# A hybrid attention encoder block on eight cores: eight buffers for x, weight loads queued behind it, a reordered last attention unit, per-block waits in the output projection, and the last tile's norm in pieces

## The chip, the cores and the metric

The kernel runs on one Trainium2 chip, on all 8 NeuronCores at once, with one program. Each core takes half of the 2048 tokens of one of four sequences as its own (1024 output rows) and reads the whole sequence for keys and values; no core talks to another. The metric is device time in microseconds of the slowest core.

## The reference

`x` is (4, 2048, 2048) float32; there is one layer. What is computed:

```python
h = rms_norm(x, norm_gain)
qa, ka, va, ga, qb, kb, vb, gb, za, zb = split(h @ w_in)      # 11776 columns
# A: 8 query heads, 2 key/value heads of 128, dense softmax attention over 2048 keys
qa, ka = axial_rotary(rms_norm(qa)), axial_rotary(rms_norm(ka))
pa = (gqa_attention(qa, ka, va) * silu(ga)) @ w_branch_a
# B: 3 groups of 4 heads, window/dilation (128,1), (512,4), (2048,16), partial rotary,
#    groups combined by their softmax denominators
pb = (dilated_mixture(rotary(qb), rotary(kb), vb) * silu(gb)) @ w_branch_b
merged = sigmoid(za + b0) * pa + sigmoid(zb + b1) * pb
y = rms_norm(x + merged @ w_out, final_norm_gain)
```

## The kernel before, in words

**Stages.** (1) Head: the transposed x comes in 16 tiles of 1 MB (`xload`, tile g = 4s+q holds 512 tokens of slice s and four of the 16 blocks of 128 channels). ACT squares each tile, four matmuls with a matrix of ones sum the squares (`head_sums`), ACT makes rsqrt by Ln and Exp, and 16 DVE operations per slice write the normalised bf16 `hT` (`head_scale`). (2) `kv_proj` projects keys (32 matmuls of 512 columns per slice) and values (64 matmuls of 256 columns per slice), and `rope_post` normalises and rotates each key or query slice. (3) Mixer A (`projA`, `attA_S`, `attA_PV`, `attA_sum`), eight heads. (4) Mixer B (`projB`, `attB_S`, `attB_PV`), twelve units of one head slot and one group; the last one is n = 11. (5) Merge (`merge_units`): for each of 16 blocks c, za, zb, wba and wbb projections into the eight PSUM banks, two sigmoids, products and a sum into `mergedT` block c. (6) Output (`out_mm`): 8 token tiles by 4 column blocks, 16 matmuls each over the blocks k of `mergedT`, then the residual add, the squares and `final_norm`.

**What sets the order.** A class `Sched` records each operation into its engine's instruction list and works out the semaphore waits from named keys; `Streams.run` (line 290) merges generators, each a stream of small steps, always taking the one whose next operation its own cost model has ready earliest, less the stream's bonus (sums 0.6, scale 0.5, posts 0.3, kv 0.1, PVB 0.06, SB 0.05, projections `pj_bonus`). So the order on every engine is fixed when the program is built, and an engine waits in that order at run time. In the model every DMA costs its source bytes over 330 GB/s plus 2 us.

**Buffers of x.** `xbs` has five (NXB = 5): two halves of `yaT`, `ybT`, `gain`, and columns 10752 to 12800 of the arena ("xb4"). Tile g+5 is loaded when `head_scale` has used tile g. All x loads, the constants and both rotary tables (1 MB each, keys "ropeC", "ropeS") are issued on SP's queue at the start; weights are issued on POOL (`w_issue`, 1 MB read as float32 and written as 512 KB of bf16, eight slots). The first four wait for x tiles 1, 2, 3, 3 (`w_issue(xbk[g])`), and two more (qa0, ga0) follow at once since `projA` asks for them; slots 6 and 7 hold the squares during the head. The matrix of ones is part of `cbf`, a constant of 336 KB loaded on POOL ahead of the weights.

**Around the end of mixer B.** `proj_all` runs `projA`, `projB` and then `merge_head`, which projects za and zb of block 0 into banks 0, 1, 2 and 7; bank 7 is taken only when the last epilogue of B (`epB` = 4) is planned. After `X.run()` come the sigmoids and `mu0[14:]`, which starts with wba of block 0.

**Output.** Each matmul of `out_mm` names all 16 keys of `mergedT` (`mkeys`), though it reads one block. `final_norm` is a DVE reduction of four sums, ACT Ln and Exp, and two DVE operations of 1024 columns, each followed by a 512 KB store on SP; the program ends by waiting for the last four stores.

## Time and profile before

| | |
|---|---|
| median of 3 runs | 1216.16 us (1214.97 to 1318.25) |
| profiled execution | 1222.34 us |
| its span, slowest core (core 5) | 1220.8 us |
| spans of the cores | 1210.8 to 1220.8 us |
| PE / DVE / ACT busy on core 5 | 1158.3 / 605.1 / 510.3 us |
| last matmul of core 5 over | 1212.5 us |

The profile is one execution; its times are from the start of the span. What the device adds around the span is 1222.34 - 1220.8 = 1.5 us. "PE" is the matmul side of TensorE, "PEld" its weight loads, "idle before" the engine's idle time ahead of a group with what ended it. The granted clock is a share of 2.4 GHz.

### The profile page before, as it was taken

The numbers are of one execution on the slowest core, as the hardware profiler recorded it, in microseconds if no ns is written. First come the engines' busy times: TensorE is split into PE (matmuls) and PEld (weight loads), VectorE is DVE, ScalarE is ACT, GpSimd is POOL, SyncE is SP. The second block draws the span as 40 slices with busy tenths as digits, with TensorE's granted clock in tenths as the row PEclk, the third lists the DMA queues.
The fourth block names the chain that finished last, engine by engine and source line by source line (L and its number), as shares of the span: only waits on it lengthen the run. The fifth ranks groups of instructions, "written<-read, shape, count | busy, mean of one in ns | idle before, by whom it ended". The sixth has DMA issues, their size and how long they took to land.

```text
span 1220.8 us, 17436 instructions; the slowest of 8 cores (1210.8 to 1220.8 us)
## 1 busy us (share of the span) xinstructions
PE 1158.3 (95%) x5876; PEld 548.2 (45%) x5876; DVE 605.1 (50%) x904; ACT 510.3 (42%) x899; POOL 79.3 (6%) x165
## 2 busy tenths in 40 slices
PE   2779999999999999999999999999999999999997
PEld 0325644444444554455454454444444444434442
DVE  0559587878877653555554646332212122122254
ACT  3345477877787643443543544221111111102222
POOL 1000100000000000000000000001111111010000
PEclk9869999999999999999999999999999999999998
DMA  9945442211132423321322330036666545349333
GB/s 233 261 141 136 72 68 35 36 30 26 33 70 36 87 38 55 65 53 35 70 53 38 67 61 5 8 60 110 106 107 111 89 75 91 67 114 250 80 139 137
DMA packets 27174, 102.15 MB, mean 84 GB/s; under 512 B 3408, under 2 KB 5456, under 8 KB 23504
## 3 DMA queue, kind: packets, MB, share of 16 engines
q0 software_dynamic: 20304, 63.27, 31.2%
q1 hardware_dynamic: 6784, 37.78, 9.2%
q8 instruction: 49, 0.80, 0.3%
q14 instruction: 37, 0.30, 0.1%
HBM read 155.90 MB, written 8.39 MB: 135 GB/s over the span
## 4 chain that ended last, share of the span: by engine, by line
PE 86%; DVE 5%; DMA 5%; issue 2%; ACT 2%; DVEq 0%; SPq 0%; ACTq 0%
PE pb L218 86%; DVE s_arena L218 2%; DVE s_hT L218 2%; DMA s_arena<-xt 2%; DMA s_gain<-xt 2%; DMA s_yaT<-xt 1%; ACT s_arena L218 1%; DVE s_gain L218 1%; ACT s_wsl L218 0%; ACT s_rs L218 0%; SPq L218 0%; DVEq L1319 0%; ACT s_gain L218 0%; DVEq L216 0%; DVE s_yaT L218 0%
## 5 line engine op out<-in xcount | busy, mean ns | idle before, releaser
L218 PE MATMUL pb<-s_hT,s_wsl 128*128 128x512 bf16 (+1 forms) x3456 | 754.7, 371 | 4.9 <-DVE s_hT L218 2.4
L218 PEld LDWEIGHTS pb<-s_hT,s_wsl 128*128 128x128 bf16 x3456 | 329.9, 98 | 382.0 <-issue 24.4
L218 ACT ACTIVATE s_arena<-pb 128x512 bf16<-128x512 f32 (+8 forms) x514 | 285.4, 577 | 287.0 <-PE pb L218 232.0
L218 DVE TENSOR_TENSOR s_arena<-pb,s_arena 128x512 f32<-128x512 f32 x96 | 77.6, 809 | 267.2 <-PE pb L218 265.2
L218 PE MATMUL pb<-s_arena 128*128 128x512 bf16 (+3 forms) x746 | 154.3, 310 | 5.2 <-DVE s_arena L218 3.1
L218 ACT ACTIVATE s_arena<-pb,s_mb 128x512 f32<-128x512 f32 x64 | 43.7, 687 | 241.8 <-PE pb L218 241.8
L218 DVE TENSOR_TENSOR s_arena<-s_arena 64x512 bf16<-64x512 f32 (+2 forms) x144 | 111.4, 773 | 19.3 <-ACT s_arena L218 12.8
L218 POOL DMA_DIRECT2D s_wsl<-w_in x92 | 48.6, 529 | 924.4 <-PE pb L218 904.5
L218 PEld LDWEIGHTS pb<-s_arena 128*128 128x128 bf16 x746 | 62.7, 98 | 65.6 <-issue 12.4
L218 DVE TENSOR_TENSOR s_arena<-s_arena,s_rope 128x512 f32<-128x512 f32 (+3 forms) x136 | 89.9, 661 | 4.1 <-DVE s_arena L218 0.2
L218 DVE TENSOR_TENSOR s_gain<-s_gain,s_arena 128x512 f32<-128x512 f32 x89 | 61.5, 691 | 22.2 <-ACT s_arena L218 15.6
L218 DVE COPY s_arena<-pb 128x512 f32<-128x512 f32 (+3 forms) x56 | 35.7, 637 | 70.4 <-PE pb L218 70.0
L218 PE MATMUL pb<-s_hT,s_arena 128*128 128x512 bf16 x256 | 61.6, 408 | 0.0
L218 PE MATMUL pb<-s_wsl,s_cbf 128*128 128x512 bf16 x64 | 25.6, 545 | 34.6 <-ACT s_wsl L218 20.9
L218 PE MATMUL pb<-s_yaT,s_wsl 128*128 128x512 bf16 x256 | 57.9, 379 | 0.0
L218 ACT ACTIVATE s_arena<-s_arena 128x512 f32<-128x512 f32 x80 | 50.3, 634 | 16.0 <-DVE s_arena L218 12.9
L218 ACT ACTIVATE s_gain<-pb 128x512 bf16<-128x512 f32 x86 | 50.2, 601 | 10.4 <-PE pb L218 10.2
L218 DVE TENSOR_TENSOR s_arena<-pb,s_rope 64x512 f32<-64x512 f32 (+1 forms) x64 | 40.8, 638 | 22.1 <-ACT s_arena L218 21.3
L218 PE MATMUL pb<-s_arena,s_cbf 128*128 128x512 bf16 (+1 forms) x158 | 47.7, 337 | 4.1 <-DVE s_arena L218 3.4
L218 DVE TENSOR_TENSOR s_gain<-s_gain 128x512 f32<-128x512 f32 (+2 forms) x59 | 40.7, 690 | 12.9 <-ACT s_gain L218 6.6
L218 PEld LDWEIGHTS pb<-s_hT,s_arena 128*128 128x128 bf16 x256 | 26.5, 103 | 34.8 <-issue 19.7
L218 PEld LDWEIGHTS pb<-s_yaT,s_wsl 128*128 128x128 bf16 x256 | 25.0, 98 | 30.2
(65 smaller groups left out, 599.3 us busy)
## 6 DMA issues: line engine op xcount, KB each, us to landing
s_wsl<-w_in POOLq DMA_DIRECT2D x92, 512.0 KB, 6.2
y<-s_arena SPq DMA_DIRECT2D x16, 512.0 KB, 2.7
s_yaT<-xt SPq DMA_DIRECT2D x7, 1024.0 KB, 8.6
s_wsl<-wba POOLq DMA_DIRECT2D x16, 256.0 KB, 4.9
s_hT<-xr SPq DMA_DIRECT2D x4, 1024.0 KB, 16.6
s_hT<-wout POOLq DMA_DIRECT2D x8, 512.0 KB, 34.2
s_ybT<-xt SPq DMA_DIRECT2D x3, 1024.0 KB, 14.2
s_gain<-xt SPq DMA_DIRECT2D x3, 1024.0 KB, 17.4
```

What stands on the lines that cost most here:

```text
L218: ins = getattr(engine, fn[0])(**fn[1])
```

## The change

Head: three more x buffers, two in the part of `hT` that holds slice 3 (each 8 blocks of 256 float32 columns, pieces of 1 KB) and one in columns 6144 to 8192 of the arena ("xb5", later the gate buffers of mixer A), with explicit tables of buffers and successors. The matrix of ones is a tile of its own set by DVE; `cbf` and the merge bias are loaded after x tile 15. Weights: two behind tiles 2 and 3, two behind tile 5, and qa0 and qa1 behind tiles 13 and 15. The rotary table comes in four pieces, one per slice, with a key each. `projA` starts after tile 9 (before: 7), takes qa0, qa1, then ga0, ga1, and the rest as before. End of B: the bonus of the projections falls to -0.15 once `pj_n` is over 19.75; `merge_head` also projects wba of block 0, with banks 3 and 4 taken after the last scores and bank 7 after the last PV instead of after the epilogue. Output: `out_mm` names `("mT", k)` alone. Last tile: the product with the gain is made ahead of the norm in four pieces, the sum of the four sums goes by an ACT copy with accumulation, and the scaling goes in four pieces of 512 columns, two on ACT and two on DVE, each with a 256 KB store. In the diff, `["cbf"]` becomes `["ones"]` wherever the matrix of ones is read, and "ropeC"/"ropeS" become `("rope", t0 // 512)` in the posts (left out below).

```diff
+        ones_t = sb("s_ones", [128, 128], BF16)
-        for h in range(8):
-            wlist.append((("qa", h), wsrc(w_in, QA0 + h * 128), 16))
-            wlist.append((("ga", h), wsrc(w_in, GA0 + h * 128), 16))
+        for nm, base, h in [("qa", QA0, 0), ("qa", QA0, 1), ("ga", GA0, 0), ("ga", GA0, 1)] + \
+                [(nm, base, h) for h in range(2, 8) for nm, base in (("qa", QA0), ("ga", GA0))]:
+            wlist.append(((nm, h), wsrc(w_in, base + h * 128), 16))
...
-        xbs += [g4(gain[:]), g4(af(10752, 12800))]
-        xbk += [["gain"], ["xb4"]]
-        NXB = len(xbs)
+        xbs.append(g4(gain[:]))
+        xbk.append(["gain"])
+        for i in range(2):
+            xbs.append(hT[:, 8 * i:8 * i + 8, 1536:2048].bitcast(F32))
+            xbk.append([("hT", k, 3) for k in range(8 * i, 8 * i + 8)])
+        xbs += [g4(af(10752, 12800)), g4(af(6144, 8192))]
+        xbk += [["xb4"], ["xb5"]]
+        XBUF = (0, 1, 2, 3, 6, 7, 4, 5, 0, 1, 2, 3, 6, 7, 0, 1)
+        XNEXT = {max(j for j in range(g) if XBUF[j] == XBUF[g]): g for g in range(8, 16)}
...
+        def rope_load(s):
+            sl = slice(512 * s, 512 * (s + 1))
+            S.dma("sp", rope[:, :, sl], ropeA_d.rearrange("a p t -> p a t")[:, :, sl], "c_rope%d" % s, writes=[rope_all[s]])
...
-        S.dma("pool", cbf[:], cbf_d, "c_cbf", writes=["cbf"])
-        for g in range(NXB):
-            xload(g)
-        for g in (1, 2, 3, 3):
-            w_issue(xbk[g])
+        MEMSET(ones_t[:], 1.0, ["ones"], eng="dve")
+        for g in range(4):
+            xload(g)
+        w_issue(XK[2])
+        w_issue(XK[3])
+        xload(4)
+        xload(5)
+        rope_load(0)
+        w_issue(XK[5])
+        w_issue(XK[5])
+        xload(6)
+        xload(7)
+        rope_load(1)
...
-                    if g + NXB < 16:
-                        xload(g + NXB)
+                    if g in XNEXT:
+                        xload(XNEXT[g])
+                        X.setf(("xl", XNEXT[g]))
+                    if g == 5 or g == 9:
+                        rope_load(2 if g == 5 else 3)
+                    if g == 9:
+                        w_issue(XK[13])
+                        w_issue(XK[15])
+                        S.dma("sp", mb[:], mb_d, "c_mb", writes=["mb"])
+                        S.dma("pool", cbf[:], cbf_d, "c_cbf", reads=XK[15], writes=["cbf"])
...
         def pj_bonus():
+            if pj_n[0] > 19.75:
+                return -0.15
             return 0.5 if pj_n[0] < at_n[0] + 1.15 else 0.0
...
         def projA():
-            yield from ge("sc", 8)
-            for h in range(8):
-                if h == 1:
-                    yield from ge("sums_done", 1)
-                    yield from ge("kv_done", 1)
+            yield from ge("sc", 10)
+            for nm, h in [("qa", 0), ("qa", 1), ("ga", 0), ("ga", 1)] + [(nm, h) for h in range(2, 8) for nm in ("qa", "ga")]:
+                if (nm, h) == ("ga", 0):
+                    yield from ge("kv_done", 1)
+                    yield from ge("sums_done", 1)
...
         def merge_head():
-            for i, nm in enumerate(("za", "zb")):
+            for i, nm in enumerate(("za", "zb", "wba")):
...
                 for s in range(2):
                     bi = ZB[i][s]
+                    pool = "pj" if bi < 3 else "S"
                     if bi == 7:
-                        yield from ge("epB", 4)
-                        yield from X.take("O", bi)
-                    else:
-                        yield from X.take("pj", bi)
-                    yield from mm16(w, s * 512, 512, bi, 0.1)
+                        continue
+                    if pool == "S":
+                        yield from ge("SB_done", 12)
+                    yield from X.take(pool, bi)
+                    yield from merge_mm(nm, w, s, bi)
+                    yield
+                if i == 1:
+                    yield from ge("PB_done", 12)
+                    yield from X.take("O", 7)
+                    yield from merge_mm(nm, w, 1, 7)
                     yield
...
             for k in range(16):
                 MM(pb[bi][:], mergedT[:, k, t * 128:(t + 1) * 128], wbig[cb][:, k, :], (k == 0), (k == 15),
-                   mkeys + [("wb", cb, k // 4)], [PS(bi)])
+                   [("mT", k), ("wb", cb, k // 4)], [PS(bi)])
...
+        def pre_gain(t, cb):
+            sl = slice(cb * 512, (cb + 1) * 512)
+            TT(ost[t % 2][:, sl], xts[t][:, sl], gain[:, sl], ALU.mult, [("xp", t, cb), "gain"], [("ost", t % 2, cb // 2), ("og", cb)])
+
+        def last_norm(t):
+            sc = stat[:, 32 + t:33 + t]
+            ACT(stat[:, 48:52], stat[:, 4 * t:4 * t + 4], AF.Copy, [("fs", t, cb) for cb in range(4)], [("fd", t)], accum_out=sc)
+            ACT(sc, sc, AF.Ln, [("fd", t), "eps"], [("fd", t)], scale=1.0 / D, bias=eps_t[:, 0:1])
+            ACT(sc, sc, AF.Exp, [("fd", t)], [("fd", t)], scale=-0.5)
+            for cb in (0, 2, 1, 3):
+                o = ost[t % 2][:, cb * 512:(cb + 1) * 512]
+                if cb < 2:
+                    ACT(o, o, AF.Copy, [("og", cb), ("fd", t)], [("og", cb)], scale=sc)
+                else:
+                    S.op("dve", "tensor_scalar", dict(out=o, in0=o, scalar1=sc, scalar2=None, op0=ALU.mult),
+                         [("og", cb), ("fd", t)], [("og", cb)])
+                otoks.append(S.dma("sp", y[t * 128:(t + 1) * 128, cb * 512:(cb + 1) * 512], o, "outl_%d" % cb, reads=[("og", cb)]))
+
-        for t in range(8):
+        for t in range(7):
             out_mm(t, 2)
             out_mm(t, 3)
             final_norm(t)
-        for tk in otoks[-4:]:
+        pre_gain(7, 0)
+        pre_gain(7, 1)
+        out_mm(7, 2)
+        pre_gain(7, 2)
+        out_mm(7, 3)
+        pre_gain(7, 3)
+        last_norm(7)
+        for tk in otoks[-8:]:
```

## Rows read from the trace of the kernel before

**Rows 1.** The page: busy tenths of PE in 40 slices of 30.5 us, core 5.
```profile
PE   2779999999999999999999999999999999999997
```
**Rows 2.** Stretches: length, busy time (instructions) by engine, granted clock, DMA share, GB/s.
```profile
0.00:125.00 125.00, 86.66 (x383) 38.71 (x384) 66.10 (x99) 58.36 (x63) 5.25 (x15) 0.89 0.69 188
125.00:400.00 275.00, 269.83 (x1323) 125.24 (x1321) 211.32 (x325) 202.74 (x378) 12.78 (x26) 1.00 0.27 45
...
783.00:800.00 17.00, 14.04 (x85) 6.38 (x84) 7.86 (x11) 3.93 (x7) 0.53 (x1) 0.91 0.18 32
...
1085.00:1098.00 13.00, 10.44 (x42) 4.24 (x40) 4.06 (x6) 0.69 (x1) 4.23 (x8) 0.87 0.67 183
```
**Rows 3.** PE's groups by shape, from 0 to 125 us.
```profile
L218 PE MATMUL pb<-s_wsl,s_hT 128*128 128x256 bf16 x146 | 17.1, 273 | 0.0
```
**Rows 4.** The chain that ended last: start us, us, what.
```profile
3.83 23.20 DMA s_arena<-xt
...
41.37 19.02 DMA s_gain<-xt
...
95.69 8.57 DMA s_yaT<-xt
...
796.14 293.67 PE pb L218 x1352
```
**Rows 5.** Stretches of 10 us in the head, columns as in rows 2.
```profile
60.00:70.00 10.00, 8.57 (x19) 2.36 (x20) 5.98 (x10) 3.27 (x4) 0.00 (x0) 0.50 0.22 73
70.00:80.00 10.00, 7.42 (x32) 2.68 (x29) 4.71 (x8) 4.79 (x4) 0.00 (x0) 1.00 0.86 275
80.00:90.00 10.00, 6.56 (x16) 2.13 (x17) 5.84 (x9) 7.33 (x8) 0.00 (x0) 0.51 0.25 75
```
**Rows 6.** Weight loads to landing: the six of 14 to 23 us, then the one of 105 us.
```profile
DMA to landing us min/median/max: 11.6/15.2/29.0
...
s_wsl<-w_in POOLq DMA_DIRECT2D x1, 512.0 KB, 5.2
```
**Rows 7.** Instructions of ACT and DVE in the head, in order of time.
```profile
20.46 1.91 ACT L218 ACTIVATE s_wsl<-s_gain 128x2048 bf16<-128x2048 f32 x1 [1.75 <-DMA s_gain<-xt]
27.22 1.91 ACT L218 ACTIVATE s_wsl<-s_arena 128x2048 bf16<-128x2048 f32 x1 [4.85 <-DMA s_arena<-xt]
29.03 0.67 ACT L218 ACTIVATE s_rs<-pb,s_eps_t 128x512 f32<-128x512 f32 x1
...
30.60 5.39 DVE L218 SCALAR_TENSOR_TENSOR s_hT<-s_yaT,s_gnt,s_rs 128x512 bf16<-128x512 f32 x8 [30.60 <-ACT s_rs L218]
...
98.18 0.74 DVE L218 SCALAR_TENSOR_TENSOR s_arena<-pb,s_qkg,s_arena 128x512 f32<-128x512 f32 x1
...
101.87 0.74 DVE L218 SCALAR_TENSOR_TENSOR s_arena<-pb,s_qkg,s_arena 128x512 f32<-128x512 f32 x1
```
**Rows 8.** PE's and ACT's instructions at the end of mixer B.
```profile
793.90 0.38 PE L218 MATMUL pb<-s_arena,s_cbf 128*128 128x512 bf16 x1 [1.10 <-DVE s_arena L218]
796.09 2.59 ACT L218 ACTIVATE s_arena<-s_arena 128x512 f32<-128x512 f32 x4 [7.34 <-DVE s_arena L218]
796.14 4.07 PE L218 MATMUL pb<-s_hT,s_wsl 128*128 128x512 bf16 x11 [1.86 <-DVE s_arena L218]
```
**Rows 9.** The first matmuls of the output projection.
```profile
1094.07 4.13 PE L218 MATMUL pb<-s_rope,s_arena 128*128 128x512 bf16 x11 [2.56 <-DVE s_arena L218]
```
**Rows 10.** DVE's last operations.
```profile
1212.58 0.69 DVE L218 TENSOR_TENSOR s_yaT<-pb,s_yaT 128x512 f32<-128x512 f32 x1 [2.70 <-PE pb L218]
...
1215.20 2.48 DVE L218 SCALAR_TENSOR_TENSOR s_arena<-s_yaT,s_stat,s_gain 128x1024 f32<-128x1024 f32 x2 [0.85 <-ACT s_stat L218]
```
**Rows 11.** The page's DMA issues: the stores of y, KB each, median us to landing.
```profile
y<-s_arena SPq DMA_DIRECT2D x16, 512.0 KB, 2.7
```
**Rows 12.** Stretches near the end: core 0's first, then core 5's, columns as in rows 2.
```profile
1180.00:1190.00 10.00, 10.00 (x48) 4.53 (x47) 5.44 (x8) 3.24 (x10) 0.00 (x0) 1.00 0.61 204
...
1200.00:1210.00 10.00, 10.00 (x40) 4.16 (x39) 5.41 (x7) 1.97 (x7) 0.00 (x0) 0.81 0.37 149
```

More of the change, by code:

```diff
@@ L372, in build_nc @@
         ident = cbf[:, 0:128]
-        ones_bf = cbf[:, 128:256]
+        ones_bf = ones_t[:]
         maskF = cbf[:, 256:768]
@@ L479, in rk @@
             return rope_all
-        rope_all = ["ropeC", "ropeS"]
+        rope_all = [("rope", s_) for s_ in range(4)]
         def g4(ap2d):
@@ L529, in head_sums @@
                     g = 4 * s + q
-                    yield from ge("xl", g + 1 - NXB)
-                    ACT(sqs[g % 2], xbs[g % NXB], AF.Square, xbk[g % NXB], [("w", 6 + g % 2)])
+                    yield from X.until(lambda: g < 8 or ("xl", g) in X.flags)
+                    n = XB[g].shape[2]
+                    ACT(sqs[g % 2] if n == 512 else sqs[g % 2].rearrange("p k (u n) -> p (k u) n", n=n), XB[g], AF.Square, XK[g],
+                        [("w", 6 + g % 2)])
                     yield
@@ L534, in head_sums @@
                         MM(pb[bank][:], ones_bf, sqs[g % 2][:, j, :], (q == 0 and j == 0), (q == 3 and j == 3),
-                           [("w", 6 + g % 2), "cbf"], [PS(bank)], inc=(j == 3))
+                           [("w", 6 + g % 2), "ones"], [PS(bank)], inc=(j == 3))
                     yield
@@ L589, in rope_post @@
             b2 = yield from X.alloc("pj")
-            MM(pb[b2][:], ones_bf, sqv[i], True, True, [("sq", i), "cbf"], [PS(b2)])
+            MM(pb[b2][:], ones_bf, sqv[i], True, True, [("sq", i), "ones"], [PS(b2)])
             X.free("sq", i)
@@ L741, in attA_S @@
         def attA_S():
-            yield from ge("sc", 15)
+            yield from ge("sc", 13)
             for i in range(4):
@@ L820, in attA_PV @@
                         if kc not in DSET:
-                            MM(pb[7][:], ones_bf, pbufs[p], pe_first, False, ["cbf", ("pbuf", p)], [PS(7)], inc=True)
+                            MM(pb[7][:], ones_bf, pbufs[p], pe_first, False, ["ones", ("pbuf", p)], [PS(7)], inc=True)
                             pe_first = False
@@ L1086, in attB_PV @@
                         lb = yield from X.alloc("O")
-                        MM(pb[lb][:], ones_bf, P_, True, True, ["cbf", pk], [PS(lb)])
+                        MM(pb[lb][:], ones_bf, P_, True, True, ["ones", pk], [PS(lb)])
                         X.free("pb", p)
@@ L1206, in build_nc, with merge_mm @@
         TKEYS = [(a, j) for a in ("swp", "bt1", "bt2", "sgb") for j in range(2)] + [("pbuf", i) for i in range(4)]
+        def merge_mm(nm, w, s, bi):
+            if nm != "wba":
+                yield from mm16(w, s * 512, 512, bi, 0.01)
+                return
+            for k in range(8):
+                MM(pb[bi][:], w[0][:, k, :], yaT[:, k, s * 512:(s + 1) * 512], (k == 0), (k == 7), [w[1]] + yakeys, [PS(bi)],
+                   inc=(k % 4 == 3))
+                if k == 3:
+                    yield
         def merge_head():
-            for i, nm in enumerate(("za", "zb")):
+            for i, nm in enumerate(("za", "zb", "wba")):
                 w = W((nm, 0), 3)
@@ L1250, in build_nc @@
         mu0 = merge_units(0)
-        for f in mu0[14:]:
+        for f in (mu0[16], mu0[18]) + tuple(mu0[19:]):
             f()
@@ L1275, in build_nc @@
                 big_piece(cb, q)
-        mkeys = [("mT", c) for c in range(16)]
         ost = [af(8192, 10240), af(10240, 12288)]
```

65 lines of the change are left out of this document (34 added, 31 removed).

## The prediction
> **What bounds the kernel now.** I read the busy slices first. PE is at 9 tenths or more in every slice but the first three and the last [rows 1], so from about 90 us on the kernel is a row of matmuls, and time can be won only where PE stands or runs slowly. The price of a matmul comes from the longest undisturbed piece of the chain: 1352 in 293.67 us [rows 4], 0.217 us for 512 columns. One of 256 columns is 17.1 us over 146, 0.117 us [rows 3]. Then the stretches. From 0 to 125 us PE did 383 matmuls [rows 2], 146 of them short: 237 x 0.217 + 146 x 0.117 = 51.4 + 17.1 = 68.5 us of work. So 56.5 us of the first 125 are lost, to idleness and to the lower clock (0.50 and 0.51 granted in two of the slices of 10 us, that is the level of 1.2 GHz, each after PE had waited [rows 5]). From 125 to 400 us PE is idle for 5.2 of 275 us [rows 2], with DVE busy for 211 and ACT for 203. Two small holes are left, at 793 to 800 us [rows 8] and at 1091 to 1098 us [rows 9], and the tail: the last add of DVE starts at 1212.58 us [rows 10] and the span ends at 1220.8.
>
> In the head the chain goes through the transfers of x: 23.2 us for the fifth tile, 19.0 us for one of the second round, 8.57 us for the last, which lands at 104.3 us [rows 4]. Yet the DMA engines are only 0.22 and 0.25 busy in 60 to 70 and 80 to 90 us, and 0.86 between [rows 5]: five buffers let the stream stop, since tile g+5 waits until tile g has been scaled.
>
> **Head, the stream.** From 70 to 80 us 275 GB/s moved at a busy share of 0.86 [rows 5], 320 GB/s when full, so a tile of 1.05 MB costs 3.28 us. The second-round tile of [rows 4] landed at 60.4 us, and by then nine tiles, both rope tables (two more of that size), cbf (about 2 us) and six weights had gone through, from about 2 us on: 60.4 - 2 - 2 - 11 x 3.28 = 20.3 us, 3.4 us a weight. After the change, ahead of and with x15 go sixteen tiles (52.5 us), three rope pieces (4.9) and four weights (13.6), and qa0 beside it (up to 3.4): with the start of 2 us 73.0 to 76.4 us, if the stream never stops. It nearly doesn't. Tiles 8 to 11 are issued as tiles 0 to 3 are scaled, before the queue has got to tile 7. Tiles 12 and 13 follow tiles 4 and 5, whose scaling starts once x7 has landed (about 43 us, then 1.9 us of squares, sums, Ln, Exp: 49), while tiles 8 to 11 keep the stream going until about 58. Tiles 14 and 15 hang on the scaling of tiles 8 and 9, at 64 to 68 us, just as x13 ends. I take 77 us for x15, 27 us earlier.
>
> The first slice gains too. Now ACT squares x4 at 27.22 us and only then makes Ln at 29.03, DVE starts at 30.60 [rows 7], though ACT had begun to square x3 at 20.46 [rows 7]. In the changed order x4 is issued behind two weights, its modelled arrival is later than the sums of x3, and Ln comes first: scaling starts at 24 to 25 us. The cost of the two weights is then on the keys: loads of weights took 11.6 to 29.0 us in this crowd and 5.2 us alone [rows 6], so the key matmuls start near 30 us and the values of slice 0 near 42 us. That is still within the loss that I count below.
>
> The Trainium skill (DMA: Bandwidth & Descriptors, section "Queues, rings and completion order") says that each DMA engine takes its queues in turn, packet by packet. The stretch of landings agrees: 29.0 us against 5.2 us. By that rule two queued weights slow x4 and x5 as much as x slows them, which the sum above has by bytes already; it would take nothing off x3.
>
> **Head, PE.** By 78 us PE can have done the sums of tiles 0 to 13 (56), keys of three slices (96), six post sums and values of two slices (128 short): 158 x 0.217 + 128 x 0.117 = 34.3 + 15.0 = 49.3 us, so 29 us are lost. Behind that wait values of slice 2 (64 short, 7.5), qa0 and qa1 (64, 13.9), keys of slice 3 (6.9), its values (7.5) and sums: 36 us of work while DVE scales slice 3 until about 94, so PE should be full from 78 on. I add 3 us for the lower clock after waits and 3 for banks: DVE has from 49 us three scalings of 10.7 us (5.39 for 8, [rows 7]) and ten posts, each 3.69 us from start to start (98.18 to 101.87, [rows 7]), 69 us without a pause until 118, and a product's bank is free only after its post has begun. DVE had 66.1 us done by 125 before [rows 2]; after the change it can have 70 by 101, so it permits a shift of 24 us and hardly more. Loss 35 instead of 56.5: 21.5 us saved. Bounds: 12 us (PE's fixed order stands behind weights that land late, or DVE holds the banks) to 32 us (a loss of 24.5, what the arrivals alone force). I take 22. cbf, mb and qkg cost nothing while x streams: cbf is then read by mixer B alone, whose work begins after mixer A's.
>
> The new DVE and ACT load by stage doesn't change, only its density between 50 and 120 us. Two tiles are written in pieces of 1 KB; no row prices such a piece of a plain load. Between no loss and twice 3.28 us per tile it is 0 to 6.6 us on the stream; I take 0 to 1, being nearest to the 4 KB pieces of the stores, 2.7 us for 512 KB with everything [rows 11].
>
> **End of mixer B.** PE waits 1.10 us before the last sum and 1.86 us for the last adds, then does 11 matmuls in 4.07 us instead of 2.39 [rows 8]: 4.6 us. With scores, then PV, ahead of the projections, PE has za, zb and wba of block 0 (80 long matmuls, 17.4 us) to lay beside the last unit's adds and the epilogue (793.9 to about 800.4). The cover is ample and the four units of the hole go. What is late next is wbb, which waits for the epilogue, some 10 us after the last PV, less than the 17 us. Bounds: 0 (the last scores come no earlier since the last query slice is itself delayed by the lower bonus) to 4.6. I take 4.
>
> **Output.** PE stands 2.56 us for the last block of `mergedT` and then runs 11 matmuls in 4.13 us [rows 9], 1.7 us over: 4.3 us, of which the clock part was not on every core. The last sum ends 3.0 us after the first output matmul can start, 15 of them take 3.25 us, so k = 15 finds its block. Bounds 2 to 4.3; I take 3.
>
> **Tail.** From 1212.58 to 1215.20 is the add, the square and the small steps; the reduction on DVE becomes an ACT operation (two hops fewer, 0.3 us). Then two DVE operations in 2.48 us [rows 10] and a store (2.7 us for 512 KB, [rows 11]) become two of 512 columns on each of two engines, about 1.3 us, and a store of half the size, issued fourth on SP. The products with the gain (0.7 us each) lie beside matmuls, the last beside ACT's square. 1.5 us; bounds 0 to 2.5.
>
> **Sum.** 22 + 4 + 3 + 1.5 = 30.5 us. Against the profiled execution: 1222.3 - 30.5 = 1191.8. That execution is 6.2 us above the median: on its slowest core the granted clock was 0.81 near the end [rows 12], some 8 us, where core 0 had 1.00. The savings don't depend on that, so 1216.2 - 30.5 = 1186 us.
>
> **Rivals.**
> A, forecast, 0.52: as above, 26 to 35 us saved, 1181 to 1190.
> B, 0.17: PE's fixed order meets late data. The planner prices a weight load at 3.2 us plus 2, the crowd makes it 12 to 29 [rows 6]; PE waits at the values of slice 0, the sums of x6 and x7 stand behind them, the scaling of slice 1 starts late, and the stream stops again. The head gives 11: 19 saved, 1197. For it: the six landings. Against: in the trace before no matmul's wait in the head ended on a weight.
> C, 0.10: pieces of 1 KB slow the stream by 6.6 us: 24 saved, 1192.
> D, 0.11: PE fills better than I lay out; loss 26, 38 saved, 1178.
> E, 0.07: the change of bonus doesn't do what it says; the last scores are planned where they were, the hole stays: 26 saved, 1190.
> F, 0.03, slower: the denser PE is granted less. Core 5 had 0.81 late in the output stage, at the same work at which core 0 had 1.00 [rows 12]. Each us at 0.81 loses 0.19. It decides from 160 us more of such a stretch (30.5 / 0.19); with 250 us the time is 1186 + 47 = 1233. Against: PE is at 9 tenths in all but four slices already [rows 1] and eats the lower grant only late, on some cores.
> The Trainium skill (TensorE: Matmul & The Clock Gate, section "Seeing it yourself") tells of a limiter that takes a die to 13/16 when three of its cores run dense matmuls and holds it there. The 0.81 is that size, but most of the span has 1.00 on all eight cores, so the trace doesn't bear the rule out for this load.
>
> **How the numbers follow.** The likeliest case gives 1186. B reaches 1197 and with a worse bound 1200, D 1178: the range 1177 to 1200 leaves about 0.15 out. Two per cent, about what a measurement tells here, is 1191.8. Faster by more: A, D, most of E and half of C, 0.76. Within: 0.21. Slower: F, 0.03.
>
> **What would show it.** x15's transfer over near 77 us (wrong if past 88); first scaling before 26 us; DMA share over 0.8 in every slice until 70 us; matmuls from 0 to 101 us worth about 66 us; DVE full from 50 to 115. No wait over 0.5 us of PE near the end of mixer B; PE's first output matmul at once; the end 6.8 us after the last matmul. The prediction is wrong if PE waits for a weight in the head by more than 5 us, or if 125 to 400 us loses what the head gained, with DVE the releaser.

## The result, and the profile after

| | before | after |
|---|---|---|
| median, runs side by side on one chip | 1214.97 us | 1204.74 us |
| ratio, 95% interval | | 0.9899 [0.9876, 0.9921] |
| span of the profiled execution, slowest core | 1220.8 us | 1202.9 us (core 3) |
| spans of the cores | 1210.8 to 1220.8 us | 1195.1 to 1202.9 us |
| matmuls from 0 to 125 us | 383 (core 5) | 432 (core 3) |

The change saves 0.0101 x 1214.97 = 12.3 us. The forecast was 1186 us, 30.5 saved, with a range of 1177 to 1200: the time lies outside it. (Some executions of each kernel are disturbed by a lower granted clock on one die; the ratios leave these out.)

The page of after, core 3, busy tenths in 40 slices of 30.1 us:

```profile
PE   2788999999999999999999999999999999999996
```

Against [rows 1] the third slice rose from 7 to 8 tenths and the fourth fell from 9 to 8: PE reaches 9 tenths only in the fifth. The stretches of core 3, columns as in [rows 2], and the short matmuls of the first:

```profile
0.00:125.00 125.00, 86.82 (x432) 44.63 (x433) 74.25 (x113) 58.93 (x64) 5.10 (x13) 0.86 0.71 188
80.00:90.00 10.00, 7.93 (x24) 2.97 (x25) 5.85 (x9) 4.18 (x3) 1.59 (x3) 0.66 0.69 173
100.00:110.00 10.00, 4.70 (x19) 2.02 (x17) 9.36 (x14) 5.75 (x12) 0.00 (x0) 0.76 0.00 0
125.00:400.00 275.00, 271.34 (x1309) 123.90 (x1308) 206.58 (x319) 206.13 (x385) 12.79 (x26) 1.00 0.28 47
766.00:783.00 17.00, 14.80 (x88) 6.73 (x87) 12.06 (x17) 9.05 (x15) 0.00 (x0) 0.90 0.00 1
...
L218 PE MATMUL pb<-s_wsl,s_hT 128*128 128x256 bf16 x192 | 24.1, 285 | 0.0
```

By the prices of [rows 3, 4], 432 matmuls of which 192 are short are 240 x 0.217 + 192 x 0.117 = 74.5 us of work, so 50.5 of 125 us are lost: 56.5 before, 35 forecast. Core 3 lost most; over the eight cores it is 45.7 to 50.5 us, and 55.7 to 58.4 before. The busy time of PE is the same as before (86.82 against 86.66 us in [rows 2]); what rose is what it did in it. The end of mixer B now comes 17 us earlier: the stretch from 766 to 783 us answers to that of 783 to 800 in [rows 2], and PE is idle for 2.2 us of it, 3.0 before, so the hole there is smaller but not gone. From 125 to 400 us PE is idle for 3.7 us, so nothing was given back there. Where PE stood in the head, the PE timeline of core 3 (start, us, instruction, idle before it and its releaser):

```profile
28.73 1.87 PE L218 MATMUL pb<-s_hT,s_wsl 128*128 128x512 bf16 x4 [5.41 <-DMA s_wsl<-w_in]
32.70 4.79 PE L218 MATMUL pb<-s_hT,s_wsl 128*128 128x512 bf16 x12 [2.11 <-DMA s_wsl<-w_in]
...
56.69 1.27 PE L218 MATMUL pb<-s_wsl,s_ones 128*128 128x512 bf16 x4 [3.50 <-ACT s_wsl L218]
...
82.07 1.87 PE L218 MATMUL pb<-s_wsl,s_ones 128*128 128x512 bf16 x4 [4.03 <-ACT s_wsl L218]
83.73 4.89 PE L218 MATMUL pb<-s_hT,s_wsl 128*128 128x512 bf16 x12
88.46 1.03 PE L218 MATMUL pb<-s_wsl,s_ones 128*128 128x512 bf16 x4
...
104.16 0.38 PE L218 MATMUL pb<-s_arena,s_ones 128*128 128x512 bf16 x1 [2.31 <-DVE s_arena L218]
107.19 1.44 PE L218 MATMUL pb<-s_arena 128*128 128x512 bf16 x3 [2.65 <-DVE s_arena L218]
108.43 4.50 PE L218 MATMUL pb<-s_wsl,s_hT 128*128 128x256 bf16 x24
```

The first two rows are waits for weights (7.5 us together), the next two are waits of the sums for the squares of x8 and x14, the rows at 104 and 107 us are a wait for a post of DVE and that of the first scores, and the last row shows the first values of slice 2. The row at 82.07 holds the fault in small: PE stands for 4.03 us at the sums of x14, while the 32 key matmuls of slice 2, whose data is nearly all scaled by then, come behind them in its list; the twelve of the next row are the first of these, and the sums of x15 (88.46) stand behind them. ACT and DVE on the same core:

```profile
53.34 0.69 ACT L218 ACTIVATE s_rs<-pb,s_eps_t 128x512 f32<-128x512 f32 x1 [0.32 <-PE pb L218]
83.34 1.91 ACT L218 ACTIVATE s_wsl<-s_yaT 128x2048 bf16<-128x2048 f32 x1 [1.42 <-DMA s_yaT<-xt]
89.64 0.69 ACT L218 ACTIVATE s_rs<-pb,s_eps_t 128x512 f32<-128x512 f32 x1 [4.38 <-PE pb L218]
...
25.05 5.39 DVE L218 SCALAR_TENSOR_TENSOR s_hT<-s_yaT,s_gnt,s_rs 128x512 bf16<-128x512 f32 x8 [23.71 <-ACT s_rs L218]
91.15 5.39 DVE L218 SCALAR_TENSOR_TENSOR s_hT<-s_arena,s_gnt,s_rs 128x512 bf16<-128x512 f32 x8 [4.83 <-ACT s_rs L218]
```

x15 lands at about 83.3 us, where its squares begin: 21 us earlier than before [rows 4], 6 later than forecast. Its squares end at 85.25, its Ln comes at 89.64 and its scaling at 91.15. So the stream gave 21 us, and the work behind it took up 12.3 at most, all edits together.

The issues on SP's queue, core 3, and two transfers of the chain that ended last:

```profile
6.64 22.75 SPq L218 DMA_DIRECT2D s_hT<-xt  x2
29.43 9.69 SPq L218 DMA_DIRECT2D s_rope<-ropeA  x1
...
19.74 12.82 DMA s_wsl<-w_in
...
72.52 7.42 DMA s_yaT<-xt
```

SP needs 22.75 us to issue x6 and x7, the tiles in pieces of 1 KB. x14 is issued at 72.52 us, since the scaling of slice 2 that frees its buffer starts only at 69.70; x13 had landed at 67.89, so the stream of x had stopped for some 4 us. The weight load took 12.82 us in the crowd, as the loads of [rows 6] did. The Trainium skill (DMA: Bandwidth & Descriptors, "Queues, rings and completion order") has the DMA engines take their queues in turn, packet by packet; this row and the 5.2 us of a load alone in [rows 6] agree.

The end of mixer B and the start of the output, PE on core 3, which answer to [rows 8, 9]:

```profile
775.53 0.39 PE L218 MATMUL pb<-s_arena 128*128 128x64 bf16 x8 [1.09 <-DVE s_arena L218]
776.71 0.38 PE L218 MATMUL pb<-s_arena,s_ones 128*128 128x512 bf16 x1 [0.78 <-DVE s_arena L218]
777.40 15.66 PE L218 MATMUL pb<-s_hT,s_wsl 128*128 128x512 bf16 x64 [0.32 <-DVE s_arena L218]
...
1082.98 2.32 PE L218 MATMUL pb<-s_rope,s_arena 128*128 128x512 bf16 x10
```

Three waits are left at the end of B, 1.09, 0.78 and 0.32 us. 64 projections follow each other behind them, in 15.66 us where 13.9 is their price, so a slow clock after the waits is left too. The output matmuls start with no wait. The tail, PE, DVE, ACT and SP on core 3, answering to [rows 10]:

```profile
1184.64 9.01 PE L218 MATMUL pb<-s_hT,s_arena 128*128 128x512 bf16 x41
...
1193.26 0.68 DVE L218 TENSOR_TENSOR s_yaT<-pb,s_yaT 128x512 f32<-128x512 f32 x1
1194.12 0.69 DVE L218 TENSOR_TENSOR s_arena<-s_yaT,s_gain 128x512 f32<-128x512 f32 x1 [0.17 <-DVE s_yaT L218]
1194.73 0.68 DVE L218 TENSOR_TENSOR s_yaT<-pb,s_yaT 128x512 f32<-128x512 f32 x1
...
1198.18 1.79 SPq L218 DMA_DIRECT2D y<-s_arena  x4
```

The stretch in which these four stores are under way, columns as in [rows 2]:

```profile
1199.00:1202.00 3.00, 0.00 (x0) 0.00 (x0) 0.00 (x0) 0.00 (x0) 0.00 (x0) 0.50 0.94 348
```

The last matmul ends at 1184.64 + 9.01 = 1193.65 us, the last add begins at 1194.73, 1.08 us later. Before it was 0.1 us later (matmul over at 1212.5, add at 1212.58 in [rows 10]). In between DVE does a product with the gain. The end comes 9.3 us after the last matmul, not the forecast 6.8.

### The profile page after: what moved, and what is told of

Same layout as the page of the kernel before. It is cut to its first block, busy times and chain, and to the rows that moved or that the text cites. A ratio compares the mean times of both kernels' runs of the same rounds, so it can differ in the third digit from the quotient of the medians.

```text
span 1202.9 us, 17462 instructions; the slowest of 8 cores (1195.1 to 1202.9 us)
## 1 busy us (share of the span) xinstructions
PE 1144.4 (95%) x5876; PEld 547.7 (46%) x5876; DVE 606.4 (50%) x910; ACT 512.1 (43%) x903; POOL 79.2 (7%) x163
## 4 chain that ended last, share of the span: by engine, by line
PE 90%; DVE 4%; DMA 3%; ACT 2%; issue 1%; SPq 0%; ACTq 0%; DVEq 0%; POOLq 0%
PE pb L218 90%; DVE s_arena L218 2%; DMA s_gain<-xt 1%; DMA s_wsl<-w_in 1%; DVE s_hT L218 1%; ACT s_arena L218 1%; DMA s_yaT<-xt 1%; DVE s_gain L218 0%; ACT s_wsl L218 0%; ACT s_rs L218 0%; DVE s_yaT L218 0%; SPq L218 0%; ACT s_gain L218 0%; ACT s_stat L218 0%; DVEq L216 0%
## 5 line engine op out<-in xcount | busy, mean ns | idle before, releaser
L218 ACT ACTIVATE s_arena<-pb 128x512 bf16<-128x512 f32 (+6 forms) x515 | 287.0, 577 | 283.2 <-PE pb L218 226.8
L218 DVE TENSOR_TENSOR s_gain<-s_gain,s_arena 128x512 f32<-128x512 f32 (+1 forms) x90 | 62.2, 691 | 22.8 <-ACT s_arena L218 15.2
L218 PE MATMUL pb<-s_hT,s_arena 128*128 128x512 bf16 x256 | 55.4, 379 | 0.0
L218 PE MATMUL pb<-s_arena,s_ones 128*128 128x512 bf16 (+1 forms) x161 | 48.6, 336 | 6.7 <-DVE s_arena L218 5.3
L218 PE MATMUL pb<-s_wsl,s_ones 128*128 128x512 bf16 x64 | 20.0, 443 | 24.3 <-ACT s_wsl L218 24.3
```

The lines of the kernel that those rows point to most:

```text
L218: ins = getattr(engine, fn[0])(**fn[1])
```

## The experiments

### Which part gives what

**Everything but the head** (d_head_old: the kernel before with the new end of B, output and tail).

```diff
-        XBUF = (0, 1, 2, 3, 6, 7, 4, 5, 0, 1, 2, 3, 6, 7, 0, 1)
+        NXB = 5      # and the head's loads, weights and constants as before
```

> The kernel before with only the three late edits (end of mixer B, output waits, last tile). Theory 1 (the head gave only 7 to 10 us, the late edits the rest): this kernel is 4 to 6 us faster than before, about 1210 us, and the changed kernel stays 7 to 9 us ahead of it. Rival (the head gave its 20 us and something later took 10 back): the late edits alone are then worth nothing or less, the time is 1215 us or over. PE's loss up to 160 us should be that of before, 53 to 54 us.

0.9944 [0.9924, 0.9963]: the late edits give 6.8 us (forecast 8.5), which leaves 0.9944 - 0.9899 = 0.0045, 5.5 us (give or take 3.6, by the intervals), to the head, forecast at 22. The ratios go by the slowest core. The mean span of all cores, over the executions that the ratios count, is 1212.4 us for before, 1206.2 here and 1198.0 for after: 6.2 us for the late edits and 8.2 for the head. Core 6 did as much in the head as the kernel before ([rows 2]):

```profile
0.00:125.00 125.00, 86.04 (x377) 37.72 (x378) 65.58 (x98) 57.83 (x62) 5.25 (x15) 0.89 0.72 188
```

The failure is in the head, on which the next section works. The three late edits, each put back alone:

**End of B as before** (d_bend_old).

```diff
-            if pj_n[0] > 19.75:
-                return -0.15
-            for i, nm in enumerate(("za", "zb", "wba")):
+            for i, nm in enumerate(("za", "zb")):
```

> The changed kernel with the end of mixer B as before. Theory: the hole of 3 us and the low clock after it come back, 3.5 to 4.5 us slower than the changed kernel, about 1208. Rival (the hole had only moved, or the merge's first block hid it): within 1 us of the changed kernel.

0.9931 [0.9913, 0.9948], 3.9 us slower than after by the ratios, whose intervals just overlap. On core 5 the waits are larger than in after:

```profile
776.30 13.35 PE L218 MATMUL pb<-s_hT,s_wsl 128*128 128x512 bf16 x48 [1.79 <-DVE s_arena L218]
792.33 5.27 PE L218 MATMUL pb<-s_hT,s_wsl 128*128 128x512 bf16 x16 [2.23 <-DVE s_arena L218]
```

**All blocks named again** (d_mkeys_old).

```diff
-                   [("mT", k), ("wb", cb, k // 4)], [PS(bi)])
+                   mkeys + [("wb", cb, k // 4)], [PS(bi)])
```

> The changed kernel with all 16 keys named by each output matmul. Theory: PE stands 2.6 us at the start of the output stage and loses up to 1.7 us more to the clock: 2.5 to 4 us slower than the changed kernel, about 1207.5. Rival (something else, such as the adds of the last block, holds the first output tile anyway): within 1 us.

0.9922 [0.9895, 0.9948]: 2.8 us by the ratios, whose intervals overlap; the row of core 5 shows the same wait as [rows 9]:

```profile
1084.06 3.61 PE L218 MATMUL pb<-s_rope,s_arena 128*128 128x512 bf16 x16 [2.56 <-DVE s_arena L218]
```

**The last tile's norm as before** (d_tail_old).

```diff
-        for t in range(7):
+        for t in range(8):
             out_mm(t, 2)
             out_mm(t, 3)
             final_norm(t)
-        pre_gain(7, 0)
...
-        last_norm(7)
```

> The changed kernel with the last tile's norm as before. Theory 1 (the products with the gain stand in DVE's queue ahead of the last adds and cost more than the pieces save): 1 us faster than the changed kernel, about 1203, and from the last matmul to the end 8.3 us instead of 9.2. Rival (the pieces save what was forecast, 1.5 us): 1.5 us slower, about 1205.5.

0.989 [0.9871, 0.991], 1203.39 us: the old tail is no slower. On core 2, DVE (last matmul over at 1193.33, span 1201.6):

```profile
1193.44 0.69 DVE L218 TENSOR_TENSOR s_yaT<-pb,s_yaT 128x512 f32<-128x512 f32 x1 [1.21 <-PE pb L218]
```

The add follows the matmul by 0.11 us. Over the cores the end comes 8.3 to 9.1 us after the last matmul here, 9.3 to 11.2 us in after. The products delay the last add by a us; the rest of the difference is behind it, where four stores go out (1.79 us for their issues on SP) instead of two. On core 3 of after these four took 2.3 to 3.1 us to land, median 2.9, for 256 KB each, against 2.7 for 512 KB in [rows 11]. They are under way together: from 1199 to 1202 us the DMA engines are 0.94 busy and move 348 GB/s, so the megabyte takes its 3 us in four pieces as in two.

**The same matmuls, stretch by stretch.** PE runs the same matmuls in all these kernels, so the start of the matmul with a given number left to run marks the same place in the work. In us, medians over the cores whose trace has all 5876 matmuls:

| | start to 5273 left (head) | to 2172 left | to 1711 left (end of B) | to 427 left (merge, start of output) | to the end |
|---|---|---|---|---|---|
| before | 160.5 | 579.1 | 91.7 | 280.7 | 100.8 |
| d_head_old | 161.4 | 578.3 | 87.2 | 277.1 | 101.7 |
| after | 152.2 | 576.2 | 89.4 | 277.1 | 102.0 |
| d_bend_old | 152.9 | 576.2 | 94.3 | 277.1 | 102.0 |
| d_mkeys_old | 152.7 | 576.3 | 89.4 | 279.8 | 101.7 |
| d_tail_old | 152.2 | 576.3 | 89.4 | 277.1 | 100.8 |

The head's edits give 9.2 us in the head and 2.1 behind it, and cost 2.2 at the end of mixer B, where the planned order came out differently with them (87.2 against 89.4; why is not shown). The edit of the end of B is worth 4.5 us in the kernel before and 4.9 in after, the output's 3.6 and 2.7, and the last tile's costs about 1.

### Why the head gives so little

Theories: the order fixed by the planner (rival B, widened from weights to all loads), the pieces of 1 KB (rival C), and DVE.

**The planner told the measured landing times** (h_model; x8 to x15 get 2 us more, which puts them 0.3 to 1.3 us ahead of their landings on core 6). The instructions are the same; only the landings in the planner's model move, so the orders do.

```diff
-        tok = (ent[0], ent[1], None, "d_" + semname, self.dma_free + 2.0)
+        tok = (ent[0], ent[1], None, "d_" + semname, at if at is not None else self.dma_free + 2.0 + late)
+        XLATE = 2.0      # all x tiles from 8 on
+        XAT = {0: 9.4, 1: 12.7, 2: 16.7, 3: 19.3, 4: 23.5, 5: 27.0, 6: 44.1, 7: 46.0}
-        w_issue(XK[2])
+        w_issue(XK[2], at=28.6)     # then 32.6, 39.0, 42.5; qa0, qa1 late=1.0
```

> The changed kernel with the same instructions; only the times at which the planner believes the head's loads to land are set to those of the changed kernel's trace (first weights 28.6 and 32.6 us instead of 18 and 21, tiles 6 and 7 44.1 and 46.0, 2 us more for the later tiles). The order on the engines in the head changes with that. Theory order (the fixed order meets late data: squares of tiles 6 and 7 behind the posts of slice 0, sums of tiles 14 and 15 around the query projections): Ln of slice 1 at about 49 to 50 us instead of 53.3, PE's waits of 3.5 us at 56 and 4.0 us at 78 gone, 4 to 8 us faster than the changed kernel. Theory supply or DVE (transfers and DVE set the pace whatever the order): within 2 us.

0.98 [0.9783, 0.9818], 1191.77 us: 12 us better than after. Core 6, stretches, short matmuls and timelines:

```profile
0.00:125.00 125.00, 94.91 (x519) 50.67 (x520) 79.83 (x121) 63.95 (x73) 6.15 (x15) 0.95 0.78 196
100.00:110.00 10.00, 9.16 (x48) 4.49 (x46) 9.22 (x15) 2.51 (x4) 0.00 (x0) 1.00 0.01 2
...
L218 PE MATMUL pb<-s_wsl,s_hT 128*128 128x256 bf16 x246 | 28.8, 273 | 0.6 <-DMA s_wsl<-w_in 0.6
...
85.67 1.02 PE L218 MATMUL pb<-s_wsl,s_ones 128*128 128x512 bf16 x4 [1.91 <-ACT s_wsl L218]
...
50.28 0.69 ACT L218 ACTIVATE s_rs<-pb,s_eps_t 128x512 f32<-128x512 f32 x1 [0.84 <-PE pb L218]
```

273 long and 246 short matmuls are 88.0 us of work: 37.0 us lost (36.3 to 40.3 over the cores), 35 forecast. Ln of slice 1 is 3 us earlier, x15's sums come 2.8 us earlier, and the stretch of 100 to 110 us, 4.70 us busy at 0.76 in after, is 9.16 busy at 1.00. SP is still held for 22.5 us by x6 and x7, and x15 lands at 83.5 us as before. The pieces are not the cause of these 12 us; the order is.

**Pieces of 4 KB** (h_pieces: x6 and x7 in the upper half of the rope tile and in two parts of the arena).

```diff
-        for i in range(2):
-            xbs.append(hT[:, 8 * i:8 * i + 8, 1536:2048].bitcast(F32))
+        xbs.append(rope[:, :, 1024:2048])
+        xbs.append(af(2048, 8192).rearrange("p (u n) -> p u n", n=3072)[:, :, 0:1024])
-                    if g == 5 or g == 9:
+                    if g == 7 or g == 9:
```

> The changed kernel with tiles 6 and 7 landing in the upper half of the rotary table's buffer and in two free parts of the arena, pieces of 4 KB instead of 1 KB. Theory pieces (a load of 1024 pieces blocks SP's queue, its issue lasted 22.8 us in the changed kernel, and with it the issue of tiles 8 to 11 at 39 to 42 us instead of 28 to 36): the issues of tiles 8 to 11 come right after the scalings of tiles 0 to 3, tile 7 lands 2 to 5 us earlier, and the time falls by 2 to 5 us. Rival (the stream is full anyway and the late issue only keeps the queue shorter): landings within 1.5 us, time within 1.5 us of the changed kernel.

No ratio. Its lowest time is 1204.25 us, where after has 1200.04 to 1204.74; the spans are 1194.8 to 1202.7 us, as in after. SP on core 4:

```profile
6.46 0.66 SPq L218 DMA_DIRECT2D s_rope<-xt  x1
7.16 2.44 SPq L218 DMA_DIRECT2D s_arena<-xt  x1
```

3.1 us of issue instead of 22.75, and 5.95 for the rope load behind them instead of 9.69. x6 lands 4.4 us earlier (38.7), x7 at 46.3 (45.8 in after), x11 1.2 us earlier, and PE's waits at 104 and 107 us are those of after (2.31 and 2.65). So SP's block is real, and no gain from its end shows here: the stream behind it had enough queued. With one time alone, a us or two is left open.

**No rotation for A's keys and the first two query heads** (h_norot; these posts end after the multiplication by the gain).

```diff
+            if skip:
+                yield from X.until(gate)
+                STT(dst, pb[bank][:], qkg[:, gc:gc + 1], stdv[j], [PS(bank), "qkg", ("std", j)], [dkey])
+                ...
+                return
```

> The changed kernel without the rotation in the posts of all keys of mixer A and of query heads 0 and 1 (3 rotary products and the sum left out, one DVE operation left of five): about 35 us less DVE work in the head. Theory DVE (DVE is full from 91 to 118 us and holds PE's banks): the waits of PE between 100 and 108 us and the low clock after them go, 5 to 8 us faster than the changed kernel. Theory supply or order (what comes before 90 us decides): 0 to 3 us faster.

0.9838 [0.9822, 0.9853], 7.4 us less than after. Core 5:

```profile
0.00:125.00 125.00, 91.56 (x465) 46.87 (x466) 51.38 (x79) 59.94 (x66) 5.62 (x14) 0.96 0.72 188
100.00:110.00 10.00, 8.62 (x43) 3.97 (x42) 5.49 (x9) 6.29 (x12) 0.00 (x0) 1.00 0.00 0
...
81.69 1.86 PE L218 MATMUL pb<-s_wsl,s_ones 128*128 128x512 bf16 x4 [3.87 <-ACT s_wsl L218]
```

DVE's posts are what the gap at 100 to 110 us ends on, since without 23 us of them (51.38 against 74.25) it nearly closes. But the waits for x14's squares stay, and the same kernel with all of DVE's work and a better order (h_model) is faster still. Its plan too was made with shorter posts, so the two causes are not cleanly parted by this run.

### Which landing time matters

**Early loads only** (m_first: the fixed times for x0 to x7 and the first four weights; nothing added for the rest).

```diff
-        XLATE = 2.0
+        XLATE = 0.0      # and no late= for qa0, qa1
```

> The changed kernel with corrected landing times for the first eight tiles and the first four weights alone; the later tiles and qa0, qa1 as the planner had them. Theory two places (4 us at slice 1, 6 to 8 us between 78 and 112 us): Ln of slice 1 at about 50 us, but PE's waits at 78 to 82 and 100 to 107 us stay; 3 to 4 us faster than the changed kernel, about 1200. Rival (the early correction sets off the whole gain): 9 us or more faster.

0.989 [0.9869, 0.9912]: nothing. Core 7:

```profile
51.23 0.69 ACT L218 ACTIVATE s_rs<-pb,s_eps_t 128x512 f32<-128x512 f32 x1 [1.52 <-PE pb L218]
...
81.76 1.87 PE L218 MATMUL pb<-s_wsl,s_ones 128*128 128x512 bf16 x4 [5.55 <-ACT s_wsl L218]
```

Slice 1 is ready 2 us sooner, and the wait at x14's squares is 1.5 us longer (5.55 against 4.03): a gain ahead of a late tile ends in the wait for it.

**Late loads only** (m_later: 2 us on x8 to x15, 1 us on qa0 and qa1).

```diff
-        XAT = {0: 9.4, 1: 12.7, 2: 16.7, 3: 19.3, 4: 23.5, 5: 27.0, 6: 44.1, 7: 46.0}
+        XAT = {}         # 2.0 for g >= 8 alone; first four weights as in after
```

> The changed kernel with the corrections of the later tiles (2 us more from tile 8 on, 1 us more for qa0 and qa1) alone. Theory two places: the waits at 78 to 82 and 100 to 107 us go, Ln of slice 1 stays at 53 us; 6 to 8 us faster than the changed kernel, about 1196. Rival (the early correction is the one that counts): within 2 us.

0.9816 [0.9798, 0.9833], 1195.14 us: 10 of h_model's 12 us. Core 4:

```profile
0.00:125.00 125.00, 94.27 (x498) 49.57 (x499) 77.73 (x118) 63.55 (x72) 6.17 (x15) 0.99 0.74 196
...
78.07 7.07 PE L218 MATMUL pb<-s_hT,s_wsl 128*128 128x512 bf16 x32
```

273 long and 225 short are 85.6 us of work, 39.4 lost (39.1 to 41.7 over the cores). Its instruction list shows how: all 32 key matmuls of slice 2 (the row at 78.07) stand ahead of the sums of x14 and x15, where PE stood idle in after, the values of slice 2 run from 92 to 103 us, and the first scores come at about 118 instead of 107 us. In after, the keys of slice 2 ended only at 101 us, and its values stood behind queries and scores that wait for DVE, from 108 to 125 us, though slice 2 was scaled by 80.4 us.

**Is it luck of the order?** The same 2 us for x8 to x15 changed to -1, +1 and +4 (l_minus, l_plus1, l_plus4); qa0 and qa1 stay 1 us later in all three, as in m_later.

```diff
-        XLATE = {g_: (2.0 if g_ >= 8 else 0.0) for g_ in range(16)}
+        XLATE = {g_: (-1.0 if g_ >= 8 else 0.0) for g_ in range(16)}
```

> As m_later, but the planner believes tiles 8 to 15 to land 1 us earlier than in the changed kernel's plan instead of 2 us later, so further from the trace. Theory order (a plan near the true landing times is what helps): no gain, within 3 us of the changed kernel or slower, 1202 to 1208. Rival luck (any shake-up of the greedy order gains as often as it loses): nothing follows from the sign, a gain like m_later's 9 us is as likely here.

> As m_later, with tiles 8 to 15 planned 1 us later. Theory order: part or all of m_later's gain, 1194 to 1201. Rival luck: anywhere between 1190 and 1210.

> As m_later, with tiles 8 to 15 planned 4 us later, later than the trace shows them. Theory order, in the form that leaning to the late side is harmless (PE is given work that is surely there): 1193 to 1199. In the form that only the true time helps: over 1200. Rival luck: anywhere between 1190 and 1210.

The planned times are those of each kernel's own planner, counted from its start; the landings are those of the core named; the last two columns are the stretches of the table above.

| x8 to x15 planned later by | ratio to before | x8 planned, landed | x15 planned, landed | head | end of B |
|---|---|---|---|---|---|
| -1 us (l_minus, core 7) | 0.9904 [0.9885, 0.9923] | 46.2, 53.4 | 72.8, 84.9 | 154.2 | 90.8 |
| 0 (after, core 3) | 0.9899 [0.9876, 0.9921] | 47.2, 53.1 | 74.8, 83.3 | 152.2 | 89.4 |
| +1 us (l_plus1, core 1) | 0.9819 [0.9801, 0.9836] | 48.2, 52.8 | 76.8, 84.9 | 149.5 | 87.2 |
| +2 us (m_later, core 4) | 0.9816 [0.9798, 0.9833] | 49.2, 52.4 | 78.8, 83.5 | 144.5 | 89.4 |
| +4 us (l_plus4, core 3) | 0.9819 [0.9795, 0.9842] | 51.2, 53.7 | 83.1, 89.7 | 147.8 | 87.2 |

Core 7 of l_minus, then core 3 of l_plus4, the same stretch, and where l_plus4 has the sums of x15:

```profile
100.00:110.00 10.00, 4.36 (x15) 1.41 (x14) 9.43 (x15) 5.80 (x11) 0.00 (x0) 0.78 0.04 8
```
```profile
100.00:110.00 10.00, 8.83 (x66) 6.08 (x64) 9.90 (x16) 3.18 (x6) 0.00 (x0) 1.00 0.40 79
...
94.33 1.02 PE L218 MATMUL pb<-s_wsl,s_ones 128*128 128x512 bf16 x4 [0.56 <-ACT s_wsl L218]
```

The ratios form a step: 1 to 4 us more all give 9 to 10 us, 0 and -1 give none. Two things limit what the step shows. Its size is not all from the head: with +1 the head's stretch gives 2.7 us and the end of B 2.2, with +2 the head gives 7.7 and the end of B nothing, with +4 it is 4.4 and 2.2. So a change of the plan also moves the order far behind the loads, and that part is not explained; luck of the order is ruled out for m_later's head, not for the equal totals. And no x8 or x15 in the table landed ahead of its plan, even with 4 us added (l_plus4's expectation takes its plan for later than the trace; by the planner's own times it is not).

l_plus4 also shows how little the arrival of x15 itself decides here. It lands at 89.7 us, its sums run at 94.33 and slice 3 is scaled from 97.89, all 6 to 7 us later than in after, and the kernel is 10 us faster.

**The same for the kernel before** (b_model: its own measured landings in its planner).

```diff
+        XAT = {0: 8.5, 1: 13.9, 2: 16.7, 3: 20.3, 4: 27.2, 5: 51.0, 6: 54.3, 7: 58.0, 8: 60.4}
-        for g in (1, 2, 3, 3):
-            w_issue(xbk[g])
+        for g, at_ in ((1, 26.0), (2, 29.0), (3, 32.9), (3, 36.5)):
+            w_issue(xbk[g], at=at_)
```

> The kernel before, with only the planner's landing times in the head set to those of its own trace. Theory supply (with five buffers the stream stops, tile 15 lands at 104 us, and no order helps much): 0 to 4 us faster than before, 1211 to 1215. Rival (the order alone was the loss, the eight buffers are not needed): 10 us or more faster than before.

1.0003 [0.9993, 1.0014]. The plan of before had x8 to x15 land 8 to 13 us earlier than they did; this one has them within 1.6 us of their landings on core 0, and nothing is gained. Core 0:

```profile
0.00:125.00 125.00, 84.68 (x400) 40.46 (x407) 67.49 (x101) 59.23 (x64) 5.25 (x15) 0.92 0.71 188
```

With five buffers these landing times bring no better order. The changed head is needed for the gain, and a better plan to collect it. Which of the head's edits is needed (buffers, order of the weight loads, rope table in pieces) was not tested one by one.

### A better tail, and the best version

**Two gain products a tile earlier** (t_fix).

```diff
-        pre_gain(7, 0)
-        pre_gain(7, 1)
+            if t == 6:
+                pre_gain(7, 0)      # behind out_mm(6, 2); pre_gain(7, 1) behind out_mm(6, 3)
```

> The changed kernel with the first two products with the gain of the last tile made before the norm of the tile before it. Theory (these two, 1.5 us, stand before the last two adds): the last add of DVE starts 0.1 us after the last matmul instead of 1.1 us after it, and from the last matmul to the end it takes 8.0 to 8.4 us instead of 9.2; time 0.8 to 1.2 us less than the changed kernel's. Rival (the last add waits for something else): from the last matmul to the end still over 9 us.

0.9885 [0.9867, 0.9902], not to be told from after. DVE on core 0:

```profile
1182.53 0.69 DVE L218 TENSOR_TENSOR s_arena<-s_yaT,s_gain 128x512 f32<-128x512 f32 x1 [1.89 <-DMA y<-s_arena]
```

The earlier product waits for the store of tile 5, whose buffer it writes. The last add is late by 0.1 us on four cores and still by 0.3 to 1.0 on the others: half a cure.

**h_model with the old norm of the last tile** (best).

```diff
         # the planner's landing times of h_model, and
-        for t in range(7):
+        for t in range(8):
```

> h_model (the planner told when the head's loads land) with the last tile's norm as before. Theory: the pieces of the last tile cost 1 to 1.5 us net in every kernel (10.0 us from the last matmul to the end in h_model, 8.3 to 9.1 with the old norm), so this is the fastest, 1190 to 1191 us, with the last add 0.1 us after the last matmul. Rival (the two effects are not additive, the end is set by the stores): 1191.5 to 1192.5.

0.9787 [0.977, 0.9805], 1191.2 us, spans 1183.7 to 1188.5 us. It beats both kernels. Against h_model (0.98) the intervals overlap, so what the old norm is worth there is shown by rows alone. In this kernel x8 to x15 landed 0.3 to 1.6 us ahead of their planned times on core 3, the only run where a plan was late. Core 3, DVE:

```profile
1178.86 0.69 DVE L218 TENSOR_TENSOR s_yaT<-pb,s_yaT 128x512 f32<-128x512 f32 x1 [1.20 <-PE pb L218]
```

## Why the prediction was wrong

**Head, 22 us forecast, 5.5 measured (8.2 on the mean of the cores); this is the step that failed.** Its first half held in kind. First scaling was to come at 24 to 25 us and came at 25.05; keys near 30, and they began at 28.73. x15 was to land at 77 and landed at 83.3, a slip of 6 us: x13 landed at 67.9, 2 to 4 us later than laid out, and "the stream never stops" failed once, since x14 was issued at 72.52 and not at 64 to 68 (the DMA engines moved 121 GB/s from 70 to 75 us). Slice 1's Ln was put at about 49 us and came at 53.34. In h_model, with x6 and x7 issued as slowly, it comes at 50.28, so 3 of these 4 us are order and not transfer. The second half, "so PE should be full from 78 on", did not hold. It counted 36 us of work whose data was there and let PE take it in any order. PE takes it in the planned order, and the plan had the tiles from x8 on landing by bandwidth plus 2 us, which was 5 to 8.5 us before they did. By the prices of [rows 3, 4] PE had lost 36.1 us by 78 us (29 forecast) and lost another 14.4 from there to 125 (6 forecast); in h_model it is 32.9 and 4.1. So the sums of x8 and x14 stood too early (waits of 3.50 and 4.03 us), the keys of slice 2 behind the sums of x14, DVE had its posts to make behind slice 3's scaling (91 to 102 us), and PE stood with the values of slice 2 behind them in its list. From 80 to 90 and 100 to 110 us it also ran at 0.66 and 0.76 of the clock after these waits. "DVE full from 50 to 115" failed likewise: 5.85 us of 80 to 90.

It is rival B's mechanism. I gave it 0.17 and 1197 us. Two parts of it were off: the head gave 5.5 (8.2 on the mean core) instead of B's 11, and B named only the weights and x6, x7 as late, while m_first shows that mending these gives nothing and m_later that the second round gives 10 us, 7.7 of them in the head's stretch. The argument held against it, that no wait in the head ended on a weight before, spoke of a kernel in which x was later than all (b_model: with true times in its plan it gains nothing). The text's own sign for being wrong, a wait of over 5 us for a weight, came true (5.41 and 2.11), but these waits were not what cost most: m_first planned for them and won nothing.

With the plan mended the sum comes out: 37.0 us lost in h_model for 35 forecast, and 24.3 us saved in all, of which 24.3 - 6.8 = 17.5 are the head's, within the bounds of 12 to 32 and 4.5 short of the 22.

**Rival C, pieces of 1 KB.** Their price is on SP's queue, 22.75 us, and hardly on the stream, which lost 1 us (x11) by h_pieces. That run has no ratio, so a us or two of time is left open.

**End of B, 4 us forecast.** 3.9 by d_bend_old, whose interval touches that of after; 4.5 to 4.9 by the stretches. So the size is right, but not by "the four units of the hole go": 2.2 us of waits and 1.8 of slow clock are left there, and "no wait over 0.5 us" failed (1.09 and 0.78). What the edit is measured against in after, 94.3 us, is itself longer than before's 91.7, and from before to after this stretch gives 2.3. Rival E, that the bonus does nothing, is out. **Output, 3 us:** 2.8, the same wait of 2.56 us back in d_mkeys_old.

**Tail, 1.5 us forecast; wrong sign.** It was said that "the products with the gain lie beside matmuls". The last two do not: they are queued on DVE between the last adds, and the last add starts 1 us late. Four stores of half the size saved nothing, since together they move the same megabyte with the DMA engines full. The undone parts together, 3.9 + 2.8 and nothing for the tail (0.989 against 0.9899), agree with the 6.8 us of all three within the intervals.

The chance of "faster by more", 0.76, is a little more than its parts add up to: 0.52 + 0.11, most of 0.07 and half of 0.10 are 0.75 at most.

**Clock, rival F.** The mean granted clock is 0.98 to 0.99 on all eight cores of after, so a denser PE was granted no less; the low grants of the head, 0.66 and 0.76 on core 3, follow waits.

Open: what part of the last 37 us of loss could go. By the prediction's arrivals 24.5 are forced, and h_norot shows DVE next in line, but no run had both h_model's plan and less work on DVE.

## What to carry to other kernels

When the order on the engines is fixed at build time, a faster transfer is worth only as much as that order can use: after any change to the loads, put measured landing times back into the planner. Here 1 to 4 us added to the planned landings of x8 to x15 won 9 to 10 us and 1 us taken off won nothing; the plans were still up to 8 us ahead of the landings, so what a load costs that is planned clearly too late was not tested. Then compare the stretches behind the loads too, since the order there moves with the plan. Before crediting an earlier arrival, list what stands behind each early instruction in its queue. At the end of a program count every instruction queued ahead of the last one on its engine, work moved off the last step included.
